# Expert rows scaled after the transpose, a masked bias table, one spread matmul per statistic and two shape register sets in an encoder layer

## The reference

```
h   = rms_norm(x, g_attn);  q, k, v = h @ w_qkv          # 16 heads of 64
qa, ka = rms_norm per head                               # heads 0-7: 8 x 16 window on a 64-wide grid, learned bias rpb
qb, kb = rope(rms_norm per head)                         # heads 8-15: three (window, dilation) bands, one softmax over all
x  += concat(rms_norm(out_a), rms_norm(out_b)) @ w_o
h2  = rms_norm(x, g_ffn)                                 # router in f32: 1 of 4 groups, then 2 of its 8 experts
x  += sum over the 2 experts e of gate_e * (silu(h2 @ w_gate[e]) * (h2 @ w_up[e])) @ w_down[e]     # width 512
x  += sigmoid(rms_norm(x, g_ple) @ w_ple_gate) * (p @ w_ple_proj)                                  # p: 256 wide
```

## Time and profile before

| | us |
|---|---|
| median of 3 runs | 4615.3 (4610.36 to 4635.99) |
| the profiled execution's own time | 4576.24 |
| its span (first to last instruction, core 1) | 4573.3 |
| spans of the 8 cores | 4473.6 to 4573.3 |
| TensorE busy | 3561.5 (78%) |
| VectorE busy | 2331.3 (51%) |
| ScalarE busy | 1808.9 (40%) |
| GpSimd busy | 491.5 (11%) |
| mean granted TensorE clock, core 1 | 0.875 |

### The profile page before, as it was taken

The page is one execution under the profiler, slowest core; times in us unless marked ns, Lnnn a source line. Parts: engine busy times, 40 slices in busy tenths (PEclk is TensorE's granted clock), DMA queues, the critical chain, the costliest instruction groups (busy, mean ns, idle before and its releaser), DMA issues.

```text
span 4573.3 us, 87528 instructions; the slowest of 8 cores (4473.6 to 4573.3 us)
## 1 busy us (share of the span) xinstructions
PE 3561.5 (78%) x36192; PEld 2097.5 (46%) x36224; DVE 2331.3 (51%) x4499; ACT 1808.9 (40%) x3195; POOL 491.5 (11%) x487
## 2 busy tenths in 40 slices
PE   2778778786887877788878789776688898886887
PEld 1344344453455443455545445444455555553333
DVE  3655565454656555556545455543222222226998
ACT  3454345252545433355534244422122322223554
POOL 0000000010100001000001010011000000005774
PEclk9888888797998888799989798856899999998999
DMA  7698896363446445255536345333689978757986
GB/s 211 154 190 192 198 193 123 94 141 99 101 86 139 103 105 134 90 96 99 125 98 146 97 80 88 106 104 118 177 224 237 250 209 219 223 166 236 263 261 203
DMA packets 496171, 706.27 MB, mean 154 GB/s; under 512 B 224416, under 2 KB 342560, under 8 KB 483232
## 3 DMA queue, kind: packets, MB, share of 16 engines
q1 hardware_dynamic: 382192, 527.73, 39.5%
q0 software_dynamic: 113584, 172.88, 21.8%
HBM read 547.17 MB, written 309.42 MB: 187 GB/s over the span
## 4 chain that ended last, share of the span: by engine, by line
PE 58%; DVE 17%; DMA 8%; ACT 7%; issue 6%; POOL 1%; another core or an unknown queue 1%; SPq 1%; DVEq 0%; POOLq 0%; ACTq 0%
PE psA L480 55%; DVE arena L508 8%; DVE arena L516 6%; ACT arena L495 6%; PE psA L483 3%; DMA arena<-nam 3%; DVE arena L505 2%; DMA y_d<-arena 1%; ACT arena L502 1%; DMA arena<-wq 1%; DMA arena<-x 1%; POOL arena L508 1%; DMA arena<-y_d 1%; DVE arena L512 1%
## 5 line engine op out<-in xcount | busy, mean ns | idle before, releaser
L480 PE MATMUL psA<-arena 128*128 128x512 bf16 (+16 forms) x33504 | 3328.6, 279 | 751.8 <-DVE arena L508 318.5
L480 PEld LDWEIGHTS psA<-arena 128*64 128x64 bf16 (+3 forms) x33504 | 1882.1, 121 | 2091.2 <-issue 1487.1
L495 ACT ACTIVATE arena<-psA 128x256 f32<-128x256 f32 (+7 forms) x1392 | 941.8, 700 | 1220.3 <-PE psA L480 1133.6
L495 ACT ACTIVATE arena<-arena 128x1024 bf16<-128x1024 f32 (+7 forms) x968 | 565.9, 593 | 643.5 <-DVE arena L516 360.5
L508 DVE TENSOR_TENSOR arena<-arena 128x1024 bf16<-128x1024 bf16 (+11 forms) x1144 | 632.1, 565 | 256.7 <-ACT arena L495 181.6
L508 DVE TENSOR_TENSOR arena<-psA,arena 128x256 bf16<-128x256 f32 (+2 forms) x704 | 350.0, 497 | 586.3 <-ACT arena L495 548.1
L502 ACT CAST arena<-psA 128x512 bf16<-128x512 f32 x512 | 296.8, 586 | 794.0 <-PE psA L480 757.3
L516 DVE SCALAR_TENSOR_TENSOR arena<-psA,arena 128x512 f32<-128x512 f32 (+1 forms) x448 | 304.0, 679 | 369.9 <-PE psA L480 350.4
L483 PE MATMUL psA<-arena 128*128 128x128 bf16 (+1 forms) x2688 | 273.3, 253 | 245.6 <-DVE arena L512 89.5
L505 DVE CAST arena<-psA 128x512 bf16<-128x512 f32 x256 | 176.9, 691 | 486.8 <-PE psA L480 468.1
L516 DVE SCALAR_TENSOR_TENSOR arena<-arena 128x512 f32<-128x512 bf16 (+4 forms) x384 | 351.0, 916 | 142.6 <-ACT arena L495 116.7
(11 more groups left out here) (20 smaller groups left out, 288.7 us busy)
## 6 DMA issues: line engine op xcount, KB each, us to landing
arena<-x SPq DMA_DIRECT2D x128, 512.0 KB, 4.1
yr_d<-arena SPq DMA_DIRECT2D x192, 256.0 KB, 4.0
wg_b<-w_eg POOLq DMA_DIRECT2D x32, 1024.0 KB
wu_b<-w_eu POOLq DMA_DIRECT2D x32, 1024.0 KB
wd_b<-w_ed POOLq DMA_DIRECT2D x32, 1024.0 KB
x_d<-arena SPq DMA_DIRECT2D x64, 512.0 KB, 4.5
arena<-wg_b SPq DMA_DIRECT2D x32, 1024.0 KB, 6.2
arena<-wu_b SPq DMA_DIRECT2D x32, 1024.0 KB, 6.9
```

The lines of the kernel that those rows point to most:

```text
L480: return lambda e: e.matmul(o, lhsT=l, rhs=rr, start=st, stop=sp, skip_group_check=True)
L495: nd = node("act", [lambda e: e.activation(out=o, in_=i, func=func, **kw)], r, w, c_act(n))
```

## The change

- The table of bias carries -1e30 where the mask is 0, so `nam`, its loads and the multiply go; exp writes the bf16 table straight.
- The norm weight `g_ffn` leaves `wo_chunk` (x times rstd is then a ScalarE op) and is applied to the transposed rows of each expert, 8 VectorE ops per expert. `gf` goes.
- The statistics' high part and rest stand on two partitions of one tile (`gv[:, 30]` is -1 on every second of them), and one matmul spreads both.
- Two sets of shape registers, one for even and one for odd experts; `expert` is recorded in three parts: the register write at e - 0.6, `expert_up` at e, `expert_down` at e + 0.5. Every matmul chain keeps the PSUM bank that its recording gave it.
- Keys: all units' projections at J - 1.15 + 0.25t, norm tiles one unit earlier, the last sequence's chunks at J + 0.3 + 0.25c.
- Rings: x 4 (was 3), xT 2 (was 1), P 5 (was 6), yE a ring of 8.
- The planner's figures: 300 instead of 220 for SP's DMAs, 90 instead of 60 ns between engines, 120 ns after ScalarE and VectorE ops.
- Host layouts: expert weights as rows of 128 partitions, `p` transposed on the host and loaded for four tiles at once, so the last part's p transposes go; its h copy moves to ScalarE.

The diff, cut to its core:

```diff
@@ -174,7 +175,7 @@
             st = max(free[k], n.ready)
             if n.nbytes is not None:
                 free[k] = st + n.dur
-                dma_free[k] = max(dma_free[k], free[k] + 1000.0) + n.nbytes / (220.0 if k == "sp" else 140.0)
+                dma_free[k] = max(dma_free[k], free[k] + 1000.0) + n.nbytes / (300.0 if k == "sp" else 140.0)
                 n.done = dma_free[k] + 1200.0
                 lat = 0.0
@@ -186,7 +187,7 @@
                 if s.left == 0:
                     heap_push(wait[s.eng], (s.ready, s.idx))
             for s in n.succ:
-                lat = 60.0 if (s.eng != k or k != "pe") else 0.0
+                lat = 90.0 if (s.eng != k or k != "pe") else 0.0
                 s.ready = max(s.ready, n.done + lat)
                 s.left -= 1
@@ -529,9 +528,11 @@
     MUL, ADD, SUB = ALU.mult, ALU.add, ALU.subtract
 
     tasks = []
+    nth = [0]
 
     def at(key, f):
-        tasks.append((key, len(tasks), f))
+        nth[0] += 1
+        tasks.append((key, nth[0], f))
 
 
@@ -594,15 +593,15 @@
     t_ring = ar.ring(3, [512], F32, "t")
     EBt, bEB = ar.alloc([2, NA_I], BF16, 1, "EB")
     EBv, bEBv = ar.alloc([2, NA_V], BF16, 1, "EBv")
-    p_ring = ar.ring(6, [2, 512], BF16, "P")
+    p_ring = ar.ring(5, [2, 512], BF16, "P")
     msk, bMsk = ar.alloc([896], BF16, 1, "msk")
     cosT, bCos = ar.alloc([S], F32, 1, "cos")
     sinT, bSin = ar.alloc([S], F32, 1, "sin")
     r_ring = ar.ring(2, [256], F32, "r")
     y_ring = ar.ring(2, [512], BF16, "y")
-    x_ring = ar.ring(3, [D], F32, "x")
+    x_ring = ar.ring(4, [D], F32, "x")
     h_ring = ar.ring(5, [D], BF16, "h")
-    xt_ring = ar.ring(1, [4, 128], F32, "xT")
+    xt_ring = ar.ring(2, [4, 128], F32, "xT")
     yl, bYl = ar.alloc([8, 512], BF16, 1, "yl")
     y2, bY2 = ar.alloc([2, 512], BF16, 1, "y2")
@@ -643,11 +642,8 @@
             n = min(1024, NA_W - o)
             stg, bS = x_ring.next()
             dma("sp", stg[:, 0:n], nab[h, :, o:o + n], [], [bS], n * 512)
-            stm, bM = x_ring.next()
-            dma("sp", stm[:, 0:n], nam[:, o:o + n], [], [bM], n * 512)
-            act(stg[:, 0:n], stg[:, 0:n], AF.Exp, [bS], [bS], n)
             e, be = h_ring.next()
-            tt(e[:, 0:n], stg[:, 0:n], stm[:, 0:n], MUL, [bS, bM], [be], n)
+            act(e[:, 0:n], stg[:, 0:n], AF.Exp, [bS], [be], n)
             dma("sp", eb_d[h, :, o:o + n], e[:, 0:n], [be], [bEbd[h]], n * 256)
 
@@ -673,7 +669,7 @@
 
     def cast_w(e, m):
         src, dst, kk, n = ((w_eg, wg_b, 8, 512), (w_eu, wu_b, 8, 512), (w_ed, wd_b, 4, D))[m]
-        dma("pool", dst[e].rearrange("p (k f) -> p k f", k=kk), src[e].rearrange("(k p) f -> p k f", p=128), [], [bWcast[e][m]], 2500000, after=pace[0])
+        dma("pool", dst[e], src[e], [], [bWcast[e][m]], 2500000, after=pace[0])
 
 
@@ -771,11 +767,11 @@
         act(rs, rs, AF.Exp, [brs], [brs], 512, scale=-0.5)
         rb, brb_ = rb_ring.next()
         vcopy(rb[:, 0, :], rs, [brs], [brb_], 512, 0.55)
-        tt(rb[:, 1, :], rs, rb[:, 0, :], SUB, [brs, brb_], [brb_], 512)
+        stt(rb[:, 1, :], rb[:, 0, :], gv[:, 30:31], rs, MUL, ADD, [brs, brb_, bGv], [brb_], 512)
         for i, (t, part, rw, br, sq, bsq) in enumerate(blocks):
             bc, bbc_ = gbank()
             bbc = [bbc_]
-            node("pe", [MM(bc, sel[:, i, :], rb[:, q, :], q == 0, q == 1) for q in range(2)], [brb_, bSel], bbc, 440.0)
+            node("pe", [MM(bc, sel[:, i, :], rb[:, 1, :], True, True)], [brb_, bSel], bbc, 220.0)
             sl = slice(512 * t, 512 * t + 512)
@@ -1011,7 +1005,7 @@
             act(h, xt, AF.Square, [bx], [bs2, bh], 1150, accum_out=s2[:, 0:1])
             act(s2[:, 1:2], s2[:, 0:1], AF.Ln, [bs2], [bs2], 120, scale=1.0 / D, bias=EPS)
             act(s2[:, 2:3], s2[:, 1:2], AF.Exp, [bs2], [bs2], 120, scale=-0.5)
-            stt(h, xt, s2[:, 2:3], gf, MUL, MUL, [bx, bs2, bGf], [bh], 1024)
+            act(h, xt, AF.Identity, [bx, bs2], [bh], 1024, scale=s2[:, 2:3])
             hs.append((h, bh))
             lb, blb = gbank()
@@ -1143,29 +1137,29 @@
     for J in range(NJ):
         s, pos = J // 8, J % 8
         if J:
-            at(J - 1 + (-0.12 if pos else 0.3), lambda J=J: load_w(J))
-            at(J - 1 + (-0.1 if pos else 0.3), lambda J=J: load_eb(J))
+            at(J - 1.27, lambda J=J: load_w(J))
+            at(J - 1.1, lambda J=J: load_eb(J))
             for t in range(4):
-                at((J - 1 + 0.25 * t) if pos else (J - 0.5 + 0.125 * t), lambda J=J, t=t: proj(J, t))
+                at(J - 1.15 + 0.25 * t, lambda J=J, t=t: proj(J, t))
         if pos == 0 and s:
             for c in range(16):
-                at(J - 0.99 + c / 32.0, lambda s=s, c=c: norm_tile(s, c))
+                at(J - 2 + 0.25 * (c // 4) + 0.06 * (c % 4) + 0.02, lambda s=s, c=c: norm_tile(s, c))
         for c in range(4):
             f = attn_na if pos % 2 == 0 else attn_dil
             for hu in range(2):
                 at(J + 0.25 * c + 0.01 + 0.125 * hu, lambda J=J, c=c, f=f, hu=hu: f(J, c, hu))
         if pos == 7:
             for c in range(4):
-                at((J + 1.3 + 0.8 * c) if s + 1 < nseq else (J + 1.0 + 0.1 * c), lambda s=s, c=c: wo_chunk(s, c))
+                at((J + 1.3 + 0.8 * c) if s + 1 < nseq else (J + 0.3 + 0.25 * c), lambda s=s, c=c: wo_chunk(s, c))
     NCAST = 32
     for i in range(NCAST * 3):
         at(0.6 + i * (NJ - 2.0) / (NCAST * 3), lambda i=i: cast_w(NE - NCAST + i // 3, i % 3))
 
     def run_tasks():
-        tasks.sort(key=lambda q: (q[0], q[1]))
-        for _, _, f in tasks:
+        while tasks:
+            i = min(range(len(tasks)), key=lambda q: (tasks[q][0], tasks[q][1]))
+            key, _, f = tasks.pop(i)
             f()
-        tasks.clear()
@@ -1194,8 +1188,8 @@
 
     regs()
     use_table("silu_and_others")
-    pregs = [nc.tensor.alloc_register(f"rn{i}") for i in range(4)]
-    shp = [nc.tensor.shape_register(i) for i in range(4)]
+    pregs = [nc.tensor.alloc_register(f"rn{i}") for i in range(NTL - 2)]
+    shps = [[nc.tensor.shape_register((NTL - 2) * q + i) for i in range(NTL - 2)] for q in range(2)]
 
     def load_expert(e):
@@ -1207,13 +1201,15 @@
                 dma("sp", w.rearrange("p a b -> p (a b)"), src[e], [bWcast[e][m]], [bw], 1048576)
             else:
                 src = (w_eg, w_eu, w_ed)[m]
-                dma("pool", w, src[e].rearrange("(k p) f -> p k f", p=128), [], [bw], 2097152)
+                dma("pool", w.rearrange("p a b -> p (a b)"), src[e], [], [bw], 2097152)
 
     hcur = {}
 
     def load_rows(e):
         h, bh = hE.next()
         node("sp", [lambda en: en.dma_start_transpose(out=h, in_=reg_d[CAP * e:CAP * e + CAP, :])], list(bReg) + Zb, [bh], 100.0, nbytes=2900000, emb=False)
+        for k in range(8):
+            ts(h[:, k, :], h[:, k, :], gv[:, 8 + k:9 + k], None, MUL, None, [bh, bGv], [bh], CAP, 0.26)
         hcur[e] = (h, bh)
 
@@ -1224,18 +1220,23 @@
         aT, ba = aE[e % 2]
 
         def setreg(en):
-            en.reg_load(pregs, regs_i[0:1, e, :])
+            en.reg_load(pregs, regs_i[0:1, e, 0:NTL - 2])
             return en.move_shape(shp, [[(1, r)] for r in pregs])
-        bShape = bSh
-        node("pe", [setreg], [bRegs], [bShape], 900.0)
+        shp = shps[e % 2]
+        bShape = bSh[e % 2]
+        at(e - 0.6, lambda: node("pe", [setreg], [bRegs], [bShape], 700.0))
+        at(e, lambda: expert_up(e, wg, bwg, wu, bwu, h, bh, aT, ba, shp, bShape))
+        at(e + 0.5, lambda: expert_down(e, wd, bwd, aT, ba, shp, bShape))
+
+    def expert_up(e, wg, bwg, wu, bwu, h, bh, aT, ba, shp, bShape):
...
-        for m in range(6):
-            yt, by = yE[m]
+
+    def expert_down(e, wd, bwd, aT, ba, shp, bShape):
+        for m in range(NTL):
+            yt, by = yE.next()
...
+    bSh = [Buf("shape"), Buf("shape")]
     for e in range(NE):
-        for z in range(0, 1):
-            at(e - 2.5, lambda e=e: load_expert(e))
-            at(e - 1.2, lambda e=e: load_rows(e))
-            at(e, lambda e=e: expert(e))
+        at(e - 2.4, lambda e=e: load_expert(e))
+        at(e - 1.1, lambda e=e: load_rows(e))
+        at(e - 0.9, lambda e=e: expert(e))
@@ -1314,11 +1315,14 @@
                     out=y, out_offset=None, in_=yr_d, in_offset=bass.IndirectOffsetOnAxis(ap=idx_all[:, ti, k:k + 1], axis=0))],
                     [bIdx[ti // 4]] + bYr, [by], 1250.0, nbytes=262144, emb=False)
                 ys.append((y, by))
-            pt, bp = pr_.next()
-            dma("pool", pt, pin[s, 128 * c:128 * c + 128, :], [], [bp], 131072)
+            if ti % 4 == 0:
+                pcur[0] = pr_.next()
+                dma("pool", pcur[0][0], pin[s, :, c:c + 4], [], [pcur[0][1]], 524288)
+            pt, bp = pcur[0]
@@ -1335,12 +1339,8 @@
             gb = g.bitcast(BF16)
             node("pe", [TR(gb[:, 128 * k:128 * k + 128], h[:, 128 * k:128 * k + 128], identb) for k in range(8)], [bh] + CON, [bg], 480.0)
             hTt, bhT = h3T.next()
```

(11 more changed lines are left out.)

70 lines of the change are left out of this document (32 added, 38 removed).

## The result

The changed kernel took 4377.7 us, the median of its three executions (the profiled one 4347.36, its span 4346.2 on core 3), against 4615.3 before. The ratio is 0.944, 95% interval 0.934 to 0.954: faster by some 5.6%. The forecast was 4300 in a range of 4120 to 4480. In some executions, whatever the kernel, the cores of one die or both were granted a lower clock and took some per cent longer: the ratios leave these out (of the changed kernel the one of 4579 us), and of a6_old_keys, b3_phased and b4_phased_rate, whose profiled executions had it on cores 0 to 3, the text reads cores 4 to 7.

The account below looks back on a forecast made before the run. The prediction saw four bounds: transfers, TensorE, low-clock chunks, and VectorE at the end. Its terms summed to -314 us, from the profiled 4576 to 4262, 4301 at the median's level; it forecast 4300, range 4120 to 4480.

Parts of the forecast that it names:

- Mask table: Start and sequence 0: dropping the mask's loads and multiplies gives -15 us (0 to -25) and -55 (-15 to -117).
- rival C: More gain: tail takes three chunks, `nam` gives all its 137 us, banks flow; about 4150 us, chance 0.14.
- Planner's figures: Whole kernel, with the rings of P and yE: they only move the fixed order, 0 us (+30 to -30).
- Spread matmul: Attention units: 256 fewer matmuls of 512 columns on TensorE, some falling into idle time, -40 us (0 to -80).
- Norm and projection tiles: First unit after a sequence's end: earlier norm tiles remove its 19 us excess, three times; -25 us (+20 to -57).
- Tail: Last four output-projection chunks: two mix with unit 31's attention and save 76 us; taken as -75 (0 to -150).
- Two shape sets: Experts: next up/gate group fills TensorE's 2.3 us wait, 0.9 us register wait vanishes; -75 us (+40 to -99).
- Row scalings: Experts: 8 new VectorE ops, 3.4 us per expert, hidden; 0 inside and +3 us once for the first expert.
- E: Rival: lower granted clock in the experts, 0.81 for 0.95, so they gain 13 for 75; 4362 us, chance 0.05.
- A: Rival: transfers bind in experts and last part, so both terms (107 us) vanish; about 4405 us, chance 0.18.
- B: Rival: planner keeps down(e) ahead of up(e+1) and the last chunks behind unit 31; 4422 us, chance 0.13.
- D: Rival: VectorE's row scalings stand waiting for the transpose, 9 us lost per expert; 4663 us, chance 0.08.

Follow-up runs that it names:

- a6_old_keys: Changed kernel with the keys of loads, norm tiles and projections as before; units 8 to 31 took 2200 us (cores 4 to 7), units 1 to 7 544.
- b3_phased: Changed kernel with the planner's old figures up to unit 30 and in the last part, and the rows' transpose figured at 1000000 bytes; ratio 0.941.
- b4_phased_rate: Changed kernel, transpose figured at 1000000 bytes, only SP's old rate 220 up to unit 30 and in the last part; units 1 to 7 547 us, last part 362.
- c1: Changed kernel with the keys of norm and projection tiles as before, loads at their new keys; units 8 to 31 took 2195 us, units 1 to 7 553.
- a1_nam: Changed kernel with the mask table, its loads and its multiply put back; 32 us dearer, units 1 to 7 594 us for 577.
- a4_no_row_scale: Changed kernel with the multiply of the expert rows by the norm weight left out; the experts' stage fell by 30 us.
- a8_rows_early: Changed kernel with the planner's figure for the rows' transpose lowered from 2900000 to 1000000 bytes; experts' stage from 870 to 853 us.
- a9_copy_dve: Changed kernel with the last part's copy of 1024 elements back on VectorE; last part from 391 to 416 us, ratio 0.962.

## Why the prediction was right, and where it was not

The direction and the range held; the forecast was 78 us below the median measured. On the own-time level the sum was -314, the profiled execution gave 4347.36 - 4576.2 = -229, the median core 4328.6 - 4528.6 = -200. That it came so near is in part luck: in units 8 to 31 the keys of the norm and projection tiles gave 50 us more than forecast or above, at a place that the prediction did not name, and covered part of what other terms gave less or cost more (mask 38 less, spread matmul 40, tail 45, scalings 27, figures 16).

Undone one at a time, the parts read against the level give: mask -32, keys of units and norm tiles -96 and +24 (c1), keys of the tail -15, second shape set -68, scalings +30, figures +16 (units 8 to 31 left out), the last part's copy -25, spread matmul 0. That is -166 of the median core's -200. The parts need not add up: by stage, some 13 us of unit 0 and 27 of the last part are in no run, while the tail's two runs give 11 more than it gained. Parts that no run undid are the casts and rings, the rule for PSUM banks, wo_chunk's norm on ScalarE and the work that left the last part.

- *Mask table, -15 and -55.* Failed. The start came (unit 0 gave 15 for the mask, of 32 in all), units 1 to 7 gave 17 of 55. The step took a share of the chain before, and half of an excess, for time that would come back. With the other edits in place the table's share is 8.2% and not 19.2, 54 us, and 17 of them came back (a1_nam). That chain time is usually inherited by the next wait stood in the prediction, under rival C, and its sum did not use it.
- *Planner's figures, 0 (+-30).* The net of +16 lies inside the range, but the zero hid effects of both signs. They cost 44 us in units 1 to 7 and 13 in the last part, gave 26 in the tail, 10 in the experts and 5 in unit 0, and cost between nothing and 30 in units 8 to 31. With the keys' 24 they turn sequence 0 from a gain of 32 to a loss.
- *Spread matmul, -40.* Failed: 0. TensorE's busy share of 0.80 was read as if work removed from it would show as time.
- *Norm and projection tiles, -25 (+20 to -57).* Too small, and at another place: -75 to -110 in units 8 to 31, +24 to +33 in units 1 to 7, in the unit where the last output-projection chunk runs and not at the boundary. The boundary unit did go from 65 to 44, but its neighbour took it back, so "no 66 us unit after a boundary" was a sign that was met and proved nothing.
- *Tail, -75.* Mis-sized: -30, of which the chunk keys are 15. Of the 16 token tiles only the first two reached their router matmuls before unit 31's last y store; the other 14 ran after it at a granted clock of 0.61, as the text had feared for two chunks.
- *Two shape sets, -75.* Right size (68), half of the mechanism. The 0.9 us of the register write went, but the 2.3 us did not close; what went instead was the wait for the copies of down's products, 18.5 us in the earlier trace rows, which the sum did not use. Of the 68 us 45 are idle time.
- *Row scalings, +3.* Mis-sized: 30. The estimate of 3.4 us of VectorE an expert was right (8 x 0.416 = 3.3). Hidden on VectorE it was not free: in the experts TensorE has 15 us more idle time with it and 24 us more at the lower level of the clock (a4_no_row_scale).
- *wo_chunk, 0.* Not tested by itself. The keys' 75 to 110 us are about all that units 8 to 31 gained (91), which leaves it little.
- *Last part, -32.* Right: -39, or about -50 with the old figures; 25 of it is the copy, the rest is in no run. The chain's lead passed to the output stores, at a DMA share of 0.83.

Among the rivals, E and A had the nearest times, 4362 and 4405 for 4378, and neither cause is seen. For A the experts would have gained nothing; they gained 41 us, at a DMA share that rose to 0.86, and without the scalings the inner part of the stage reached 0.91. That shares much over 0.81 do occur stood in the earlier trace rows already, 0.86 in sequence 0. B was half right: down(e) does stay ahead of the first group of e+1. D exists in the kernel of a8_rows_early, at 3 us an expert and not 9; in the changed kernel VectorE's idle time before its scalings is 3.2 us in 600. For E, the granted clock in the experts was 0.94 for 0.95, with TensorE busy 754 of 858 us on the profiled core. By the peak-current rule of the Trainium skill ("TensorE: Matmul & The Clock Gate", Part 1: The HAM clock gate), 13/16 of the clock once three cores of a die run dense matmuls, it would have been 0.81; this trace does not agree. The value itself does occur: in the profiled execution of b3_phased core 3 was granted 0.81 from 3100 to 3900 us, where core 4, in the same stage of the same kernel, was granted 0.97. What decides between them no run here shows.

## What to carry to other kernels

Where the order is fixed by a planner, its figures are part of the change: undo them alone before crediting any edit, and try them by stage. A load's share in the chain of waits is a poor price for its removal: here 137 us in the chain before (start and sequence 0) came to 32 us of time, and beside the other edits the share was already less than half in sequence 0. Undoing the edit alone in the changed kernel gives the price, and that kernel's chain shows who stands beside it. And read a stage's gain as a median over the cores at marks of the work, with the edit's untouched stages as the measure of scatter: in most stages it tells 10 us apart where the whole run could not tell 40. In the long attention stretch that holds only on like cores of one chip; comparing four cores of one run with eight of another gave an apparent 58 us of which 49 were the cores'.

## What the runs showed of the hardware

A tensor_scalar on 128x768 bf16 in SBUF took 0.416 us on VectorE, where one of 1024 elements from f32 to bf16 took 0.749. A PSUM copy of 1024 bf16 elements took 1.00 us on ScalarE and 0.69 on VectorE. In units 8 to 31 the same kernel took different times on the two dies of a chip, and which was longer went with the chip: cores 0 to 3 28 to 61 us longer in the four kernels of one chip, cores 4 to 7 41 to 71 us longer in three of another and 37 in a9_copy_dve on a third. After a wait of 2.48 us in which TensorE was idle, its granted clock was 0.57 for 4 us and then 1.00. With 256 matmuls of 512 columns more, TensorE had a mean granted clock of 0.879 to 0.888 where three kernels on the same chip had 0.860 to 0.882, and the time was no longer.
